# Index queries in two matmuls instead of three for 128 token rows, and two of eight convolution channel blocks on GpSimd, in a four-layer fp32 forward pass

## The reference, cut to what matters

```python
qi = apply_rope_2(qi.reshape(b, s, 16, 128), cos, sin)      # 2048 columns of w_in
ki = apply_rope_2(ki.reshape(b, s, 1, 128), cos, sin)[:, :, 0]
wi = wi * 16 ** -0.5 * 128 ** -0.5
for start in range(0, 256, 128):                             # two blocks of 128 tokens
    rel = einsum('bthd,bsd->bhts', qi[block], ki[:, :end])
    score = einsum('bhts,bth->bts', relu(rel), wi[block])
    score = where(causal, score, -1e30)
    _, idx = top_k(score, 64)                                # top_k = 256 // 4
    ...                                                      # attention over the selected keys
u = a * sigmoid(gt)                                          # 1024 channels
y = causal depthwise convolution of u, 31 taps, + conv_b     # then layer norm and silu
```

## Time and profile before

| | us |
|---|---|
| median of 3 runs (lowest to highest) | 2985.41 (2984.69 to 2985.76) |
| span of the profiled execution | 2982.8 |
| median less that span | 2.6 |
| busy in the span: PE, DVE, ACT, POOL | 2965.0, 2538.7, 2235.4, 8.3 |

### The profile page before, as it was taken

The page is one execution under the profiler, slowest core; times in us unless marked ns, Lnnn a source line. Parts: engine busy times, 40 slices in busy tenths (PEclk is TensorE's granted clock), DMA queues, the critical chain, the costliest instruction groups (busy, mean ns, idle before and its releaser), DMA issues.

```text
span 2982.8 us, 38320 instructions
## 1 busy us (share of the span) xinstructions
PE 2965.0 (99%) x13671; PEld 2478.2 (83%) x13671; DVE 2538.7 (85%) x4060; ACT 2235.4 (75%) x3809; POOL 8.3 (0%) x21
## 2 busy tenths in 40 slices
PE   8999999999999999999999999999999999999998
PEld 7888888878888888888888888888888888888887
DVE  6767679799888799999888888888998998888887
ACT  8798886966778676798885557777669989555684
POOL 0000000000000000000000000000000000000000
PEclk9999999999999999999999999999999999999999
DMA  9655555665556565555665666666565665666565
GB/s 328 194 174 174 173 194 192 202 185 179 176 183 205 164 219 170 175 173 183 183 195 183 204 205 205 210 192 199 153 196 174 184 184 180 190 203 206 181 205 176
DMA packets 305839, 570.35 MB, mean 191 GB/s; under 512 B 18368, under 2 KB 45152, under 8 KB 305264
## 3 DMA queue, kind: packets, MB, share of 16 engines
q1 hardware_dynamic: 301728, 557.65, 59.7%
q10 hardware_dynamic: 3040, 6.42, 0.6%
q0 software_dynamic: 880, 3.83, 0.4%
HBM read 565.73 MB, written 2.10 MB: 190 GB/s over the span
## 4 chain that ended last, share of the span: by engine, by line
PE 95%; ACT 3%; issue 1%; DVE 1%; DMA 0%; DVEq 0%; SPq 0%; ACTq 0%
PE gp L152 84%; PE bk L152 11%; ACT G L167 2%; ACT wh L167 1%; DVE wl L178 0%; DMA raw<-in_w_in 0%; DMA raw<-in_ev_w_mem_kv 0%; PE bk L155 0%; ACT tmp L167 0%; ACT nat L167 0%; DVE merged L231 0%; DVE nat L184 0%; DVE merged L178 0%; DVE nat L178 0%; DVE merged L191 0%
## 5 line engine op out<-in xcount | busy, mean ns | idle before, releaser
L167 ACT ACTIVATE wh<-raw 128x1024 fp32r<-128x1024 f32 (+2 forms) x1138 | 1149.6, 1024 | 584.6 <-PE gp L152 472.1
L178 DVE TENSOR_TENSOR wl<-raw,wh 128x1024 fp32r<-128x1024 f32 (+2 forms) x1138 | 1320.3, 1176 | 298.7 <-ACT wh L167 291.9
L152 PE MATMUL gp<-wh,Hh 128*128 128x512 f32 (+3 forms) x2121 | 822.6, 388 | 0.3 <-DVE wl L178 0.3
L152 PE MATMUL gp<-wh,Hl 128*128 128x512 f32 (+3 forms) x2121 | 814.6, 384 | 0.0
L152 PE MATMUL gp<-wl,Hh 128*128 128x512 f32 (+3 forms) x2121 | 814.6, 384 | 0.0
L152 PE MATMUL gp<-wh,Yh 128*128 128x512 f32 (+2 forms) x1762 | 684.4, 388 | 9.4 <-DVE wl L178 9.4
L152 PE MATMUL gp<-wh,Yl 128*128 128x512 f32 (+2 forms) x1762 | 679.8, 386 | 0.0
L152 PE MATMUL gp<-wl,Yh 128*128 128x512 f32 (+2 forms) x1762 | 679.7, 386 | 0.0
L152 PEld LDWEIGHTS gp<-wh,Hh 128*128 128x128 f32 x2121 | 398.6, 188 | 79.3 <-DVE wl L178 1.4
L152 PEld LDWEIGHTS gp<-wh,Hl 128*128 128x128 f32 x2121 | 398.4, 188 | 78.1
L152 PEld LDWEIGHTS gp<-wl,Hh 128*128 128x128 f32 x2121 | 398.6, 188 | 76.6
(11 more groups left out here) (173 smaller groups left out, 2270.3 us busy)
## 6 DMA issues: line engine op xcount, KB each, us to landing
raw<-in_w_in SPq DMA_DIRECT2D x544, 512.0 KB, 4.2
raw<-in_ev_w_in SPq DMA_DIRECT2D x104, 512.0 KB, 3.8
raw<-in_od_w_in SPq DMA_DIRECT2D x80, 512.0 KB, 3.9
raw<-in_w_out SPq DMA_DIRECT2D x64, 512.0 KB, 5.0
raw<-in_ev_w_out SPq DMA_DIRECT2D x40, 512.0 KB, 4.8
raw<-in_od_w_out SPq DMA_DIRECT2D x36, 512.0 KB, 4.1
raw<-in_w_b_out SPq DMA_DIRECT2D x32, 512.0 KB, 5.0
raw<-in_w_a_out SPq DMA_DIRECT2D x32, 512.0 KB, 4.9
```

What stands on the lines that cost most here:

```text
L152: return self.e.matmul(out, l, r, start=start, stop=stop)
L167: return self.e.activation(out, in_, func, **kw)
L178: return self.sketch(157 + size(a) * 1.042) if self.e is None else self.e.tensor_tensor(out, a, b, op)
```

## The change

For t = 0 of a `qi` gemm only tokens 64 to 127 are computed. One stationary operand of 128 columns holds their high parts (columns 0 to 63) and their remainders (64 to 127); it takes two matmuls, with `wh` and with `wl`. The two halves of the result are turned and roped side by side and added by a new DVE step `fold`, which packs the queries of two heads into one operand of 128 columns, so that the scores of the first block take one matmul for two heads. DVE copies the operand once a layer (`halves`), POOL loads a rope table for it (`load_half`). In `evac` the scale of this tile becomes 1.0, and the norm's factor goes into the weights `wi`. Taps of blocks 2 and 3 go to POOL: for each k two tensor_scalar and, for k > 0, one tensor_tensor over both. `mean_sum` and `center` wait for them there. `RANKS` gets `'fold': 6`. The planner gets estimates for POOL's operations, and all engines' orders are planned anew.

```diff
 def products(gm, k, t, s):
+        if gm.half and not t:
+            both = P.both(gm.L)[:, k, :]
+            e.matmul(o, both, wh, k == 0, False)
+            return e.matmul(o, both, wl, False, k == gm.nk - 1)
         e.matmul(o, lh[:, gm.lo + k, a], wh, k == 0, False)
...
 def score(l, h):
-        e.matmul(b[:, 0:128], q[:, 0:128], P.kiT[:, 0:128], True, True)
-        e.matmul(b[:, 128:384], q[:, 128:256], P.kiT, True, True).then_inc(*P.p_s.up((l, h)))
+        if h % 2 == 0:
+            e.matmul(b[:, 0:128], q[:, h % 4, 0:128], P.kiT[:, 0:128], True, True)
+        e.matmul(b[:, 128:384], q[:, h % 4, 128:256], P.kiT, True, True).then_inc(*P.p_s.up((l, h)))
 def relu(l, h):
+        c = slice(128 * (h % 2), 384)
+        e.activation(P.tmp.buf(("i", l, h))[:, c], P.bank.buf(("i", l, h))[:, c], ACT.Relu).then_inc(*P.a_relu.up((l, h)))
...
+    def tap(l, c0, k):                      # in pool_program
+        to = P.acc_pool if not k else P.tap_pool
+        if not k:
+            e.wait_ge(*P.a_glu.at(*((l, c0 // 4, a) for a in range(4))))
...
+        for i in range(2):
+            c = c0 + i
+            wk = P.cc[:, 8 * k + c:8 * k + c + 1]
+            bias, add = (P.cc[:, 248 + c:249 + c], ALU.add) if not k else (None, None)
+            x = e.tensor_scalar(to[:, i, :], P.glu[:, c, k:k + 256], wk, bias, ALU.mult, add)
...
+        x.then_inc(*P.g_tap.up((l, c0, k, "mult")))
+        e.wait_ge(*P.g_tap.at((l, c0, k, "mult")))
+        out = P.acc_pool if k < 30 else P.cv[:, c0:c0 + 2, :]
+        e.tensor_tensor(out, P.acc_pool, P.tap_pool, ALU.add).then_inc(*P.g_tap.up((l, c0, k)))
...
+    def halves(L, i):                       # in dve_program, i = 0 (high) and 1 (remainder)
...
+        e.copy(P.both(L)[:, :, 64 * i:64 * i + 64], P.pairs["H"][L][i][:, :, 64:128]).then_inc(*P.v_half.up((L, i)))
+    def fold(g):
...
+        pairs = q.rearrange("p (j i) c -> p j i c", i=2)
+        to = pairs[:, :, 0, 0:128].rearrange("p j (i c) -> p j i c", i=2)
+        e.tensor_tensor(to, pairs[:, :, :, 0:64], pairs[:, :, :, 64:128], ALU.add).then_inc(*P.v_fold.up(g))
+    def rope_half(g, part):                 # the same four operations and sizes as rope for t = 0
...
 def weights_i(l):
-        e.tensor_scalar(P.wi, P.wi, 16 ** -0.5, 128 ** -0.5, ALU.mult, ALU.mult).then_inc(*P.v_wi.up(l))
+        e.tensor_scalar(P.wi[:, 0, :], P.wi[:, 0, :], P.rs[:, 0:1], 2048 ** -0.5, ALU.mult, ALU.mult).then_inc(*P.v_wi.up((l, 0)))
+        e.tensor_scalar(P.wi[:, 1, :], P.wi[:, 1, :], 16 ** -0.5, 128 ** -0.5, ALU.mult, ALU.mult)
+        e.wait_ge(*P.v_wi.at((l, 0)))
+        e.tensor_copy(P.wi[0:64, 0, 1:16:2], P.wi[64:128, 0, 0:16:2]).then_inc(*P.v_wi.up(l))
 def accumulate(l, h):
-        for t, c in ((0, slice(0, 128)), (1, slice(128, 384))):
...
+        if not h:
+            e.tensor_scalar(P.acc[0:64, first], s[0:64, first], w[0:64], None, ALU.mult)
+            e.scalar_tensor_tensor(P.acc[64:128, first], s[64:128, first], w[64:128], P.masks[64:128, 0, first], ALU.mult, ALU.add)
+        elif h % 2 == 0:
+            e.scalar_tensor_tensor(P.acc[:, first], s[:, first], w, P.acc[:, first], ALU.mult, ALU.add)
...
 def top_start(l):                           # two more small DVE operations: shift the even heads' half, add
+        e.tensor_copy(P.work[64:128, 0:128], P.acc[0:64, 0:128]).then_inc(*P.v_top.up((l, "shifted")))
...
+        e.tensor_tensor(P.work[64:128, 0:128], P.work[64:128, 0:128], P.acc[64:128, 0:128],
+                        ALU.add).then_inc(*P.v_top.up((l, 0)))
 def top_end(l):                             # one more: the plain causal mask for tokens 0 to 63
+        e.tensor_copy(P.work[0:64, 0:128], P.masks[0:64, 0, 0:128]).then_inc(*P.v_top.up((l, "sel")))
...
 def conv_half(gm):
-                add("dve", "tap", l, c0, k)
+                add("pool" if c0 in TAPS_BY_POOL else "dve", "tap", l, c0, k)     # TAPS_BY_POOL = (2,)
```

More of the change, by code:

```diff
@@ L21 @@
 LEAD_BLOCKS = 7
-RANKS = {'duo_copy': -1, 'duo_middle': -1, 'duo_outer': 0, 'duo_inner': -1, 'duo_end': -1, 'evac_duo': 3, 'evac': 0, 'merge': 0, 'load_tanh': 3, 'tap': 6, 'center': 6, 'conv_norm': 6, 'conv_scale': -1, 'conv_silu': 6, 'zb': 1, 'weighs': -1, 'flip_x': 1, 'gate': 2, 'scale_p': 1, 'rope': 0, 'softplus': 0, 'var_sum': 0, 'refine': 3, 'flip_y': -1, 'zb_move': 1, 'flip': 2, 'log_keep': 0, 'a_strict': -1, 'move_x': 1, 'stick_out': -1, 'turned': 1, 'recip': 6, 'yb_hi': -1, 'glu_move': 2, 'top_round': -1, 'head_out': 0, 'in_lo': 1, 'log_after': 3, 'smax': -1, 'square_in': 3, 'flip_glu': -1, 'flip_p': 1, 'yb_lo': -1, 'aexp': 3, 'move_y': 1, 'relu': 2, 'residual': 2, 'log_beta': 2, 'stat': 0, 'root': -1, 'exp': 2, 'move_x_dve': 3, 'move': 2, 'duo_residual': 6, 'last_duo_residual': -1, 'weigh': 0}
+RANKS = {'fold': 6, 'duo_copy': -1, 'duo_middle': -1, 'duo_outer': 0, 'duo_inner': -1, 'duo_end': -1, 'evac_duo': 3, 'evac': 0, 'merge': 0, 'load_tanh': 3, 'tap': 6, 'center': 6, 'conv_norm': 6, 'conv_scale': -1, 'conv_silu': 6, 'zb': 1, 'weighs': -1, 'flip_x': 1, 'gate': 2, 'scale_p': 1, 'rope': 0, 'softplus': 0, 'var_sum': 0, 'refine': 3, 'flip_y': -1, 'zb_move': 1, 'flip': 2, 'log_keep': 0, 'a_strict': -1, 'move_x': 1, 'stick_out': -1, 'turned': 1, 'recip': 6, 'yb_hi': -1, 'glu_move': 2, 'top_round': -1, 'head_out': 0, 'in_lo': 1, 'log_after': 3, 'smax': -1, 'square_in': 3, 'flip_glu': -1, 'flip_p': 1, 'yb_lo': -1, 'aexp': 3, 'move_y': 1, 'relu': 2, 'residual': 2, 'log_beta': 2, 'stat': 0, 'root': -1, 'exp': 2, 'move_x_dve': 3, 'move': 2, 'duo_residual': 6, 'last_duo_residual': -1, 'weigh': 0}
 X_BY_DVE = (("x", 1), ("x", 2), ("x", 3))
@@ L33 @@
 BY_DMA = ()
+TAPS_BY_POOL = (2,)
 DUOS = ('gate2', 'gate3', 'out3', 'out2', 'out0', 'ub1_2', 'ub1_3', 'hqk7_1')
@@ L177, in tensor_tensor @@
     def tensor_tensor(self, out, a, b, op):
-        return self.sketch(157 + size(a) * 1.042) if self.e is None else self.e.tensor_tensor(out, a, b, op)
+        if self.e is None:
+            return self.sketch(200 + size(a) * 2.2 if self.plan.step.engine == "pool" else 157 + size(a) * 1.042)
+        return self.e.tensor_tensor(out, a, b, op)
     def scalar_tensor_tensor(self, out, a, s, b, op0, op1, total=None):
@@ L188, in tensor_scalar @@
         if self.e is None:
-            return self.sketch(157 + size(a) * 0.8)
+            return self.sketch(200 + size(a) * 0.9 if self.plan.step.engine == "pool" else 157 + size(a) * 0.8)
         if op1 is None:
@@ L387, in __init__ @@
         self.turns, self.targets, self.rope, self.copier, self.moved = [], [], None, "act", False
-        self.duo, self.third = None, 0
+        self.duo, self.third, self.half = None, 0, False
 class Duo:
@@ L467, in place @@
         self.acc_tap = [M[:, 2304:2560], M[:, 2560:2816]]
+        self.acc_pool, self.tap_pool = (M[:, a:a + 512].rearrange("p (c t) -> p c t", c=2) for a in (2816, 3328))
         self.csq = M[:, 2304:3328].rearrange("p (c t) -> p c t", t=256)
@@ L485, in place @@
         self.wi = g1[:, 256:288].rearrange("p (t h) -> p t h", t=2)
-        self.work = g0[:, 0:384]
+        self.work, self.half_tab = g0[:, 0:384], g0[:, 384:512]
         self.acc, self.strict = self.masks[:, 1, :], self.masks[:, 2, :]
@@ L506, in signals @@
         self.s_strict, self.s_ones = sig("s_strict"), sig("s_ones")
-        self.s_cc = sig("s_cc")
+        self.s_cc, self.s_half = sig("s_cc"), sig("s_half")
+        self.g_tap = sig("g_tap")
+        self.v_half, self.v_fold = sig("v_half"), sig("v_fold")
         self.s_out = [sig(f"s_out{i}") for i in range(4)]
@@ L694, in tables @@
                 turned(gm, R0["qk"[qb % 2]], 0, 4)
+                gm.half = True
                 self.qi[l].append(gm)
@@ L889, in free_sums, with both, tapped @@
         return [self.v_in.at(("y", 13, 2), *(("m", 0, i) for i in range(0, 16, 2)))]
+    def both(self, L):
+        return self.pairs["Y"][L][0][:, 8:16, :].rearrange("p a (b c) -> p (a b) c", c=128)
+    def tapped(self, l, *cs):
+        by = [c for c in cs if c // 2 * 2 in TAPS_BY_POOL]
+        got = [self.g_tap.at(*((l, c // 2 * 2, 30) for c in by))] if by else []
+        rest = [c for c in cs if c not in by]
+        return got + ([self.v_tap.at(*((l, c, 30) for c in rest))] if rest else [])
     def sums_of(self, gm):
@@ L1319, in load_cc, with load_half @@
         e.dma_start(P.ones, I["c_ones"]).then_inc(*P.s_ones.up(l, 16))
+    def load_half(l):
+        e.behind("load_cc", l)
+        e.wait_ge(*P.p_mm.at(P.last_sums(("gate", 2) if l else ("ub", 2))))
+        e.dma_start(P.half_tab, I["c_half"]).then_inc(*P.s_half.up(l, 16))
     def pad(l):
@@ L1326, in pad @@
         e.memset(P.glu[:, :, 0:30], 0.0).then_inc(*P.g_pad.up(l))
-    return {"zero": zero, "clear_halves": clear_halves, "load_dil": load_dil, "load_constants": load_constants, "load_gfin": load_gfin, "load_second": load_second,
-            "load_cc": load_cc, "pad": pad, "merge_add": merge_add}
+    def tap(l, c0, k):
+        to = P.acc_pool if not k else P.tap_pool
```

(100 more changed lines are left out.)

6 lines of the change are left out of this document (2 added, 4 removed).

## The result

| | median us (lowest to highest) | ratio to before, 95% interval |
|---|---|---|
| before | 2985.17 (2984.69 to 2985.76) | |
| changed | 3018.41 (3017.54 to 3018.95) | 1.011 (1.0098 to 1.0122) |

The account below looks back on a forecast made before the run. PE, busy 2965.0 of 2982.8 us, was taken to bound the kernel. 2982.8 less 32.5 of PE work plus 3 of waits gives 2953.3 of span; with 2.6 around it, 2956 us, range 2948 to 2995.

Parts of the forecast that it names:

- What POOL does to DVE: In the 60 to 150 us after 1024 and 2028: DVE loses under 20 us a layer, PE waits 3 us.
- the 20 of cover: What DVE can lose unseen a layer, from idle time and five units of lead: about 20 us.
- rival (1): POOL and DVE shut each other out when reading SBUF; decides from 36 us a layer on; 3007 us, chance 0.21.
- a memset that reads nothing: The trace's one overlap of POOL and DVE: beside it two DVE operations keep 1.29 us; called weak evidence.
- The signs that the prediction named for this: Between 1024 and 1200, tens of us of PE waits for `wl`; means of `wl` and taps rise only while POOL works.
- PE's terms: In both layers, 128 matmuls fewer in `qi` gemms, 29.0 us, and smaller score products, 3.5 us: 32.5 us in all.
- DVE by itself follows: In the index stretch DVE must do about 59 us of work and PE leaves some 80, so DVE keeps up.
- Rival (3): Newly planned DVE and ACT orders make an `lo` 3 us late in each of eight index gemms; 2977 us, chance 0.10.
- POOL's own time: POOL's multiplications and additions for the taps take 59 us a layer, hidden because the sum is needed 413 us later.

Follow-up runs that it names:

- writes_only: The changed kernel in the same planned order, with POOL's tensor_scalar and tensor_tensor replaced by memsets of the same outputs, so POOL reads nothing: 2956.69 us.
- index_only: The changed kernel with all taps back on DVE, so only the shortened index queries remain: 2990.04 us, ratio 1.0016.

## Why the prediction was wrong

**The step that failed** is in "What POOL does to DVE": "I take a loss under 20 us, which leaves PE 3 us of scattered waits". From the rows of 1024 to 1178 us, means against the earlier trace rows (0.98 us for the `wl` of 800, by its row with POOL silent): 42 x 0.251 + 61 x 0.233 + 8 x 0.31 + 6 x 0.38 = 29.5 us in four groups, in one layer. With the smaller groups the loss is some 35 to 40 us, and DVE's busy time against writes_only gives 38, past the 20 of cover and past the 36 at which rival (1) decides. The 20 itself was near: PE waited 21.5 us a layer longer, so some 16 of the 38 stayed unseen. In all, POOL's reads cost 61.7 us where the forecast had 3. The error was to let a memset that reads nothing stand for reads, and to hold that DVE loses only its surplus. The signs that the prediction named for this came: PE waited 22.2 us for `wl` between 1024 and 1200 us, and both means rose there and only while POOL worked.

**Rival (1)** had mechanism, place and sign. It gave 54 us for POOL's effect, the runs 61.7; its 3007 is 11 us short. That its size came so near is luck in part: it let all of POOL's reads hold DVE in full and had 47 us a layer lost, where the tensor_scalar by themselves took 7.5 us a layer and 38 were lost in all, and it had no term for PE's longer busy time, 19.7 us in both layers, of which some 14 are the half clock behind waits.

**PE's terms** held: 160 instructions fewer, and with POOL's reads out of the way 2956.69 us, 28.6 less than before for 32.5 summed. PE's busy time fell by 31.3 us, and waits of 12.5 us in place of 9.9 take back 2.6.

**"DVE by itself follows"** held only with the 25 us of taps taken off. Without that my own terms give 379.4 + 5.7 - 2.1 = 383 of 397 us, 96%, and index_only shows that this wants another order: 2990 with the inherited ranks, 2958 with new ones. I had costed the two parts as one, and so did not see that the first without the second does not fit the inherited order. Rival (3), a bad plan, named a cause that index_only shows at work, but was wrong in place: the waits stand not in the index gemms but behind the end of the convolution, over 350 us later.

**POOL's own time**: I took 1.22 us for the addition and 0.36 for the multiplication. The shortest additions took 1.26; the four tensor_scalar for k = 0 had a mean of 0.74, the other 120 of 1.66 with 0.91 for the shortest. How much of the rest is waiting for DVE no run shows, since DVE was busy beside all of them. POOL was busy 146 us a layer and not 59, still in time for the sum. By the estimate from the Trainium skill's "GPSIMD Engine Reference" ("Performance versus the Vector engine") the addition would be 1.1 us; measured is 1.26 at the shortest and 1.51 on average.

## What to carry to other kernels

Before work is moved from DVE to POOL, set what it takes off DVE against what POOL's instructions hold there: here a tap of two blocks on POOL relieved DVE of 0.81 us and took 1.23 from it (76.0 us over 62 of them), with up to 1.1 at a single meeting, so the trade lost at both doses and in both places tried. POOL's one-input operations cost DVE 0.12 us each, which its cover hid. When a change shortens the bounding engine's work, check that low-ranked filler on its feeders still ends in time, and replan the order before adding relief; try each part of a combined change alone.

## What was not expected of the hardware

POOL's tensor_scalar of 256 elements barely hurt DVE (15.0 us of DVE's time for 124 of them, and 1.6 us of the kernel's), and 120 of them took 1.66 us each themselves where the shortest took 0.91, while a tensor_tensor of 512 delayed a single DVE operation by 1.1 us. After a wait of 9.27 us PE ran at half clock for about 3.5 us; all such stretches make some 14 of the 61.7 us.
